# Three edits to an encoder block's first norm, last output block and first gather

## The reference

```python
def rmsnorm(x, g):
    y = x * lax.rsqrt(jnp.mean(x * x, axis=-1, keepdims=True) + 1e-5)
    return y * g

h = rmsnorm(x, norm1_g)
proj = h @ w_in + b_in                      # q, k, v of both branches, two gates
merged = sigmoid(ga) * (oa @ w_up_a) + sigmoid(gb) * (ob @ w_up_b)
x = x + merged @ w_out
h2 = rmsnorm(x, norm2_g)
logits = h2 @ w_router + b_router
gates = softmax(top_k(logits, 4))
# per chosen expert: ((clip(up) + 1) * glu(min(gate, 7))) @ w2 + b2, weighted by its gate
x = x + moe(h2)
out = rmsnorm(x, final_g)
```

## Time and profile before

| | |
|---|---|
| three runs | 1123.39, 1123.51, 1126.78 us; median 1123.51 us |
| the profiled execution | 1124.16 us; 1122.0 us from its first to its last instruction; mean granted clock 0.999 |
| TensorE busy | 1066.5 us (95%), first matmul at 5.48 us |
| VectorE, ScalarE, GpSimd busy | 303.5, 114.0, 43.1 us |
| moved | 436.05 MB, mean 389 GB/s |

### The profile page before, as it was taken

How to read it: one execution, slowest core, us unless ns; L and a number is a source line. 1 busy time by engine, 2 the same in 40 slices (tenths; PEclk the granted TensorE clock), 3 DMA queues, 4 the chain that set the end, 5 groups by cost and what they waited for, 6 DMA issues and landing times.

```text
span 1122.0 us, 13354 instructions
## 1 busy us (share of the span) xinstructions
PE 1066.5 (95%) x5293; PEld 475.6 (42%) x5293; DVE 303.5 (27%) x656; ACT 114.0 (10%) x243; POOL 43.1 (4%) x44
## 2 busy tenths in 40 slices
PE   8999999999999999999999999999999999999996
PEld 6888888633333333333333333333333333333332
DVE  4356634322222222222222222222121112222213
ACT  1042520200000000000000000000000000000001
POOL 1105500000000000000000000000000000000000
PEclk9999999999999999999999999999999999999999
DMA  9953369599999999999999999999999999999996
GB/s 357 420 211 128 113 252 389 205 379 430 428 428 426 430 428 428 429 429 427 429 429 429 428 429 428 427 430 429 428 429 429 428 428 429 429 428 429 429 422 243
DMA packets 35783, 436.05 MB, mean 389 GB/s; under 512 B 4432, under 2 KB 4944, under 8 KB 6992
## 3 DMA queue, kind: packets, MB, share of 16 engines
q1 hardware_dynamic: 34752, 434.77, 92.5%
q10 hardware_dynamic: 1008, 0.95, 0.3%
HBM read 434.66 MB, written 1.05 MB: 388 GB/s over the span
## 4 chain that ended last, share of the span: by engine, by line
PE 78%; DMA 13%; DVE 3%; SPq 3%; ACT 1%; issue 1%; another core or an unknown queue 1%; POOL 0%; POOLq 0%; DVEq 0%
PE bank L860 32%; PE bank L922 17%; DMA ring<-in_w 13%; PE bank L595 5%; PE bank L836 5%; PE bank L786 4%; PE bank L792 3%; SPq L364 3%; PE bank L696 2%; PE bank L678 2%; PE bank L539 2%; DVE work L1329 2%; PE bank L591 1%; PE bank L764 1%; PE bank L517 1%; PE bank L643 1%
## 5 line engine op out<-in xcount | busy, mean ns | idle before, releaser
L860 PE MATMUL bank<-ring,work 128*64 128x512 f32 x2048 | 451.0, 593 | 21.2 <-DMA ring<-in_w 20.7
L860 PEld LDWEIGHTS bank<-ring,work 128*64 128x64 f32 x2048 | 147.6, 137 | 304.0 <-issue 273.6
L922 PE MATMUL bank<-ring,work 128*64 128x512 f32 x1024 | 233.8, 598 | 17.5 <-DVE work L1329 17.5
L922 PEld LDWEIGHTS bank<-ring,work 128*64 128x64 f32 x1024 | 67.9, 136 | 141.0 <-issue 115.7
L1319 DVE TENSOR_SCALAR work<-bank 128x512 f32<-128x512 f32 x32 | 22.1, 692 | 388.3 <-PE bank L860 388.3
L1501 ACT ACTIVATE work<-work 128x512 f32<-128x512 f32 x32 | 20.1, 629 | 723.2 <-DVE work L1319 723.2
L836 PE MATMUL bank<-work 64*128 64x512 f32 x256 | 63.6, 615 | 1.3 <-DVE work L1299 1.3
L786 PE MATMUL bank<-x2n,work 128*64 128x512 f32 x256 | 61.9, 604 | 0.8 <-DVE work L1234 0.8
L1245 DVE TENSOR_TENSOR work<-bank,vec 128x256 f32<-128x256 f32 x64 | 24.2, 419 | 134.5 <-PE bank L792 134.5
L792 PEld LDWEIGHTS bank<-cst,work 128*128 128x128 f32 x320 | 33.8, 140 | 54.1 <-issue 50.3
L595 PE MATMUL bank<-ring 128*128 128x256 f32 x240 | 54.2, 382 | 0.0
(11 more groups left out here) (194 smaller groups left out, 572.1 us busy)
## 6 DMA issues: line engine op xcount, KB each, us to landing
ring<-in_w SPq DMA_DIRECT2D x184, 2048.0 KB, 41.5
ring<-in_w_in SPq DMA_DIRECT2D x16, 1024.0 KB, 24.1
ring<-in_w SPq DMA_DIRECT2D x15, 1024.0 KB, 13.2
ring<-in_w_out SPq DMA_DIRECT2D x4, 1024.0 KB, 4.9
ring<-in_w_up_a SPq DMA_DIRECT2D x2, 1024.0 KB, 9.6
ring<-in_w_up_b SPq DMA_DIRECT2D x2, 1024.0 KB, 6.2
ring<-in_na_rpb SPq DMA_DIRECT2D x1, 1536.0 KB, 18.2
ring<-in_w SPq DMA_DIRECT2D x2, 512.0 KB, 29.4
```

The source lines that it names most:

```text
L860: last = pe.matmul(bank[CAP * a:CAP * (a + 1), bk, :], kT, pairs[:, pair_of(par, k // 2), at + q * 512:at + (q + 1) * 512], start=False, s ...
L922: last = pe.matmul(bank[CAP * a:CAP * (a + 1), BH, :], fT, pairs[:, pair_of(par, c), at + a * 512:at + (a + 1) * 512], start=f == 0, stop= ...
```

## The change

The first norm's two column products become one product of a 128 x 128 matrix of ones by `sq_sum`, which leaves the sum of all 256 tokens on every partition. VectorE and GpSimd then work on 128 x 256 in `kraw`, and the diagonal matrices, their products and the copy go. The sums of squares of tiles 0 and 6 are taken within the last output block, ahead of `k` = 4 and `k` = 6. The first gather is made in two halves of 256 columns, into banks `BX` and `BH`; its first half starts with the first pick, ScalarE copies each half by itself, and two transposes wait for each. The counting products move behind the first expert's `k` = 0, and `count_blocks` behind `scale_gathered(0)`.

```diff
@@ gpsimd
-            power(0, slice(0, MT), 1)
+            pool.wait_ge(msq_ready, 1)
+            pool.tensor_tensor(kraw[:], kraw[:], minus_half[:, 0:1].to_broadcast([P, T]), ALU.pow).then_inc(rstd_ready, 1)
@@ tensor: first norm
                 pe.wait_ge(sq_sum_ready, 1)
-                for m in range(MT):
-                    last = pe.matmul(bank[:, BQ, m:m + 1], sq_sum[:, m * P:(m + 1) * P], ones[:, 0:1], start=True, stop=True)
-                last.then_inc(ssq_done, 1)
-
-            def spread_scale():
-
-                pe.wait_ge(diag_ready, 1)
-                for m in range(MT):
-                    last = pe.matmul(bank[:, BR, m * P:(m + 1) * P], ones[:], diag[:, m, :], start=True, stop=True)
-                last.then_inc(scale_done, 1)
+                pe.matmul(bank[:, BQ, 0:T], ones[:], sq_sum, start=True, stop=True).then_inc(ssq_done, 1)
@@ project()
-                        if c == 1 and (a, k) == (1, 4):
-                            spread_scale()
@@ out_block()
                 for k in ks:
+                    if (b, k) == (KD - 1, 4):
+                        pe.wait_ge(x2_summed, KD - 3)
+                        square_product(0)
+                    if (b, k) == (KD - 1, 6):
+                        square_product(KD - 2)
@@ tensor: after the last output block
-            pe.wait_ge(x2_summed, KD - 3)
-            square_product(0)
-            square_product(KD - 2)
             router_product(1)
             square_product(KD - 1)
@@ tensor: ahead of the first gather, the two counting products
-            for m in range(MT):
-                last = pe.matmul(bank[0:E, BH, 0:1], chosen[:, m, :], ones_16[:, 0:1],
-                                 start=m == 0, stop=m == 1)
-            last.then_inc(count_done, 1)
@@ outer_product()
+                    if first and k == 0:
+                        count_chosen()
                     if first and k in LIST_K:
                         list_blocks(LIST_K.index(k))
@@ tensor: first gather
-            pe.wait_ge(pick_ready, 1)
             pe.wait_ge(x2n_ready, MT)
-            gather()
-            pe.wait_ge(xg_ready, 1)
-            turn_gathered()
+            for hf, bk in enumerate((BX, BH)):
+                for m in range(MT):
+                    if hf == 0:
+                        pe.wait_ge(pick_ready if m else first_pick_ready, 1)
+                    for a in range(2):
+                        cols = slice(a * 512 + hf * T, a * 512 + (hf + 1) * T)
+                        last = pe.matmul(bank[CAP * a:CAP * (a + 1), bk, 0:T], pick[:, m, :], x2n[:, m, cols],
+                                         start=m == 0, stop=m == 1)
+                last.then_inc(xg_done if hf else first_part_done, 1)
+            for j in range(4):
+                if j % 2 == 0:
+                    pe.wait_ge(first_part_ready if j == 0 else xg_ready, 1)
+                last = pe.transpose(quarter(BX)[:, j, :], xg[:, j * P:(j + 1) * P], C("ident"))
+            last.then_inc(xgT_done, 1)
@@ vector: first norm
-                dve.tensor_scalar(msq[:, 0, :], bank[:, BQ, 0:MT], 1.0 / D, EPS, ALU.mult, ALU.add).then_inc(msq_ready, 1)
-                dve.wait_ge(ident_landed, 16)
+                dve.tensor_scalar(kraw[:], bank[:, BQ, 0:T], 1.0 / D, EPS, ALU.mult, ALU.add).then_inc(msq_ready, 1)
                 dve.wait_ge(rstd_ready, 1)
-                for m in range(MT):
-                    last = dve.tensor_scalar(diag[:, m, :], C("ident"), rstd[:, 0, m:m + 1], None, ALU.mult)
-                last.then_inc(diag_ready, 1)
-                dve.wait_ge(scale_done, 1)
                 dve.wait_ge(xg1_ready, KD)
-                ch.link(dve.tensor_copy(kraw[:], half_(BR)[:, 0, :]))
@@ vector: first pick and counting
-            make_pick(bass.ds(0, 1))
+            make_pick(bass.ds(0, 1), first=True)
...
+            scale_gathered(0)
             count_blocks()
-            scale_gathered(0)
@@ scalar: first gather
-            copy_gathered(0, first=True)
+            act.wait_ge(first_part_done, 1)
+            act.activation(xg[:, 0:T], bank[:, BX, 0:T], ACT.Identity).then_inc(first_part_ready, 1)
+            act.wait_ge(xg_done, 1)
+            act.activation(xg[:, T:2 * T], bank[:, BH, 0:T], ACT.Identity).then_inc(xg_ready, 1)
```

More of the change, by code:

```diff
@@ L182, in build_block @@
         sq_sum = arena[:, prob_at + 2048:prob_at + 2048 + T]
-        diag = arena[:, prob_at + 2048 + T:prob_at + 2048 + 2 * T].rearrange("p (m t) -> p m t", m=MT)
         b1_raw = arena[0:PARTS * E, prob_at:prob_at + 2 * FF]
@@ L230, in build_block @@
         xg1_ready, square_done, sq_sum_ready = sem("xg1_ready"), sem("square_done"), sem("sq_sum_ready")
-        ssq_done, diag_ready, scale_done = sem("ssq_done"), sem("diag_ready"), sem("scale_done")
+        ssq_done = sem("ssq_done")
         hT_scaled = sem("hT_scaled")
@@ L238, in build_block @@
         b1_split = sem("b1_split")
+        first_part_done, first_part_ready, first_pick_ready = sem("first_part_done"), sem("first_part_ready"), sem("first_pick_ready")
         half_landed = [sem(f"half_landed{n}") for n in range(4)]
@@ L312, in build_block @@
         BS, BT, BO, BK = 3, 5, 7, 3
-        BF, BQ, BR = 4, 6, 7
+        BF, BQ = 4, 6
         UPB = [4, 2, 0, 6]
@@ L699, in out_block, with square_product @@
                     last.then_inc(chunk_used if b % 2 else out_block_done, 1)
+            def square_product(b):
+                pe.wait_ge(x2_sq_ready, b + 1)
+                for m in range(MT):
+                    last = pe.matmul(bank[:, SSQ, m:m + 1], sq_tile(b)[:, m * P:(m + 1) * P], ones[:, 0:1],
+                                     start=b == 0 and m == 0, stop=b == KD - 1, skip_group_check=True)
+                if b == KD - 1:
+                    last.then_inc(x2_ssq_done, 1)
             def turn_x2(b):
@@ L730, in _ @@
                     router_product(0)
-            def square_product(b):
-                pe.wait_ge(x2_sq_ready, b + 1)
-                for m in range(MT):
[L736 to L739, removed]
-            pe.wait_ge(x2_summed, KD - 3)
-            square_product(0)
-            square_product(KD - 2)
             router_product(1)
@@ L805, in add_b2, with count_chosen @@
                                   b2_sb[rows, a * 512:(a + 1) * 512], start=False, stop=False, skip_group_check=True)
+            def count_chosen():
+                for m in range(MT):
+                    last = pe.matmul(bank[0:E, BH, 0:1], chosen[:, m, :], ones_16[:, 0:1],
+                                     start=m == 0, stop=m == 1)
+                last.then_inc(count_done, 1)
             def list_blocks(step):
@@ L1229, in _, with make_pick @@
             dve.wait_ge(kept_consts_landed, 16)
-            def make_pick(col):
+            def make_pick(col, first=False):
                 for m in range(MT):
@@ L1235, in make_pick @@
                                              ALU.is_equal, ALU.mult)
+                    if first and m == 0:
+                        last.then_inc(first_pick_ready, 1)
                 last.then_inc(pick_ready, 1)
-            make_pick(bass.ds(0, 1))
+            make_pick(bass.ds(0, 1), first=True)
             def scale_gathered(b):
@@ L1488, in _, with copy_gathered @@
             last.then_inc(top_exp, 1)
-            def copy_gathered(b, first=False):
+            def copy_gathered(b):
                 act.wait_ge(xg_done, b + 1)
-                if not first:
-                    act.wait_ge(hid_ready, b)
+                act.wait_ge(hid_ready, b)
                 act.activation(xg, bank[:, BX, :], ACT.Identity).then_inc(xg_ready, 1)
             act.sem_inc(scatT_ready, 1)
-            copy_gathered(0, first=True)
+            act.wait_ge(first_part_done, 1)
+            act.activation(xg[:, 0:T], bank[:, BX, 0:T], ACT.Identity).then_inc(first_part_ready, 1)
+            act.wait_ge(xg_done, 1)
+            act.activation(xg[:, T:2 * T], bank[:, BH, 0:T], ACT.Identity).then_inc(xg_ready, 1)
             def expert_block(b, last_one=False):
```

## The result

The changed kernel takes 1163.76 us (median of 5 runs, 1162.00 to 1164.47) against 1123.39 us before (5 runs): ratio 1.0359, 95% interval 1.0348 to 1.037. That is 40.4 us more; 1162.4 was forecast, and the median lies in the forecast case's own range of 1156 to 1167.

A forecast was written before the change was run, and what follows sets the result against it. TensorE's early work, then weight transfers, bound the kernel, so early delays reach the end one to one. Scale +37.1, clock +1.7, squares +0.47, gather -0.33 made +38.9 us: 1162.4 us forecast, range 1122 to 1167.

The forecast's parts named there:

- the forecast case: Whole kernel with the power at 159 ns an element: 1162 us, own range 1156 to 1167 us, chance 0.63.
- The ring's lead: Twelve 2 MiB weight slots: lead is not banked beyond them, so nothing of the 37 us is given back.
- TensorE's saved work: First norm: one 256-column product replaces column sums and spreading products, 0.78 to 0.43 us, saving 0.35 us.
- The power: First norm on GpSimd: 256 elements at 159 ns each after the first, 41.1 us; lower bound 1.2 us.
- rival (a): First norm: the long power runs near an addition's pace, 1.2 to 3.5 us; 1123.3 us, no change; chance 0.26.
- the middle pace (b): First norm: power at 40 ns an element, 10.7 us, wait 7.2 us, total 1131 us; chance 0.09.
- The start of chunk 2: First chunk needing scaled activations: TensorE starts it at about 59.8 us against 22.68 before, +37.1 us.
- The clock: After TensorE's 37 us standstill: a lower clock for a time costs 1.7 us, the middle of nothing and 3.46.
- The threshold of 3.5 us: Ahead of chunk 2: for a power of X us TensorE waits X - 3.5 us.
- Part 2: Squares' products moved into the last output block: +0.47 us on the path, bounds -0.25 to +0.5.
- Part 3: Split first gather: first expert product 0.65 us earlier, moved counting products cost 0.32, net -0.33 us.
- The sum: Whole kernel: +37.1 (scale) + 1.7 (clock) + 0.47 - 0.33 = +38.9 us.

The follow-up runs named there:

- sqrt_norm: The changed kernel with the 128x256 power replaced by a square root on ScalarE and a reciprocal on VectorE: 1123.27 us, ratio 1.0000.
- power_widths: The kernel before with GpSimd powers of 1 to 96 elements per partition added where it is idle, results unused: 1124.31 us in a single run.
- power_32: The changed kernel with the power on only 32 of the 256 tokens, the others unscaled by it: 1125.51 us, ratio 1.002.
- busy_in_wait: The changed kernel with 84 products, whose results nobody reads, put into TensorE's wait for the scale: 1163.25 us, ratio 1.0357.

## Why the prediction was right, point by point

- **What bounds the kernel.** Right. The ring's lead gave nothing back: a shift of 40.51 us at the first experts is still 40.3 us at the last long transfer.
- **TensorE's saved work, 0.35 us.** 0.45 us by `sqrt_norm`.
- **The power, 41.1 us from a slope of two points.** 41.14 us. The choice between the ends 1.2 and 41.1 us, on which all hung and which stood at 0.63, was right, and `power_widths` shows the line from 1 to 96 elements. The rule of the Trainium skill ("GPSIMD Engine Reference", section "Elementwise — side-by-side cycle accounting"), about 2.6 cycles an element for two inputs, fits the additions in the earlier trace rows nearly (2.4 ns an element) and not this operation (158.7 ns): rival (a) and the middle pace (b) both fall.
- **The start of chunk 2, +37.1 us.** +37.7. The step that was short is the first multiplication, priced at 0.63 us by the row in which GpSimd stood idle. I had moved GpSimd's additions behind the power and said that they cost nothing, thinking of who waits for them, not of whom they run beside. They made it 1.43 us, 0.8 more; only 0.6 of it shows in the +37.7, since the power ended at 58.75 us and not at 59.0.
- **The clock, 1.7 us** in the middle of 0 and 3.5. Chunk 2 took 2.2 us longer, and the clock by itself costs 2.24 us, so the mechanism was right and the size 0.5 short. That the sum stayed so near is in part luck: VectorE's slowed scaling, which the prediction did not have, costs 2.38 us by itself (0.8 ahead of chunk 2, the rest within it), and most of that lay under the half clock. Together the two are worth 2.9 us.
- **The threshold of 3.5 us.** `power_32` stands by it: TensorE waited 1.79 us for chunk 2, where 1.9 us of excess were set. The norm's stretch grew by some 0.85 us more than that excess and the saved work give, with the multiplications slowed there too.
- **Part 2, +0.47 us.** +0.78, and beyond my upper bound of 0.5. An insertion costs more than its own 0.34 us: the block went from 3.46 to 4.37 us for two, 0.45 each, since the four instructions behind each take 0.97 to 0.99 instead of 0.87. And the router's products no longer follow a busy TensorE but start 0.14 us after VectorE is done.
- **Part 3, -0.33 us.** -0.21. The first product came 0.50 and not 0.65 us earlier: the gather began 0.46 us after the first pick's start instead of 0.32. The counting cost 0.29 us, for which 0.32 was set.
- **The sum, +38.9 us.** The traces say 40.5, the medians 40.4. The 1.5 us missing are 0.6 (the start of chunk 2), 0.5 (its length), 0.3 (part 2) and 0.1 (part 3). The stated range, 1122 to 1167 us, was wide because it held the rivals too; the forecast's case alone was good to 1.4 us.

## What to carry to other kernels

Two widths of the same instruction give a start and a slope; before an operation is made wide, read the slope from its own rows and not from those of its neighbours. A small operation on [128, 2] that costs 0.7 us can be the reason that a roundabout way (a diagonal matrix and a second product) was there. And where a late instruction ends, look at what was queued behind it on its engine: it now runs beside other work than before.

## What the runs showed that I had not expected

- VectorE's 128x512 multiplications and GpSimd's 128x384 additions slow each other: four take 5.62 us beside the additions and 2.50 us without, and eight additions take 9.62 us instead of 7.87. The power took 41.14 to 41.16 us in each of the kernels, with TensorE idle or multiplying beside it. VectorE stood idle in all of these; in `power_widths` it was busy for 21.46 of the 47 us beside the powers, and they kept to their line.
- The granted clock went to 0.50 from 60 us on although TensorE had worked without a gap until 57.8 us and paused for 1.88 us only (`busy_in_wait`); in `power_32`, with a wait of 1.79 us ahead of chunk 2, it stayed at 1.00 in each window from 20 to 30 us. What makes the difference these runs don't settle.
- A reciprocal of 128x256 on VectorE takes 1.75 us, four times the 0.42 us of a multiply-add of that size.
